# Norms turned by a product with a diagonal matrix of reciprocal roots

## The reference

```python
def rms_norm(x, g):
    x32 = x.astype(jnp.float32)
    y = x32 * lax.rsqrt(jnp.mean(x32 * x32, axis=-1, keepdims=True) + EPS)
    return (y * g.astype(jnp.float32)).astype(x.dtype)

# a layer of the first stack
h = rms_norm(x, norm_mix_pre[l]);  mix = hybrid_mixer(h, ...)
x = x + rms_norm(mix, norm_mix_post[l])
h = rms_norm(x, norm_ffn_pre[l])
x = x + rms_norm(swiglu(h, w_ffn_in[l], w_ffn_out[l]), norm_ffn_post[l])

# a layer of the second stack
x = x + mixer_block(rmsnorm(x, norm_mix[l]), ...)
x = x + cross_attention(rmsnorm(x, norm_xattn[l]), rmsnorm(mem, norm_mem[l]), ...)
x = x + squared_relu_mlp(rmsnorm(x, norm_mlp[l]), w_up[l], w_down[l])
```

## Time and profile before

| | us |
|---|---|
| Runs of the kernel before | 2557.05, 2556.69, 2553.71 (median 2556.69) |
| The profiled execution | 2554.51 |
| Its span, first to last instruction | 2552.4 |
| Mean granted TensorE clock over the span | 0.968 of 2.4 GHz |
| TensorE busy (matmul) | 2371.9, 17164 instructions |
| VectorE busy | 1431.7 |
| ScalarE busy | 1093.0 |
| GpSimd busy | 48.5 |

### The profile page before, as it was taken

One profiled execution on the slowest core, in us unless ns is written; L12 is line 12 of the kernel. 1 busy time (PEld: TensorE's weight loads), 2 busy tenths in 40 slices (PEclk: granted clock), 3 DMA queues, 4 the chain that ended last, 5 costly groups with the idle time before them and its releaser, 6 DMA issues. The chain is left out here.

```text
span 2552.4 us, 40497 instructions
## 1 busy us (share of the span) xinstructions
PE 2371.9 (93%) x17164; PEld 2216.8 (87%) x17164; DVE 1431.7 (56%) x1573; ACT 1093.0 (43%) x1356; POOL 48.5 (2%) x49
## 2 busy tenths in 40 slices
PE   6999998998799999899759999989987999998996
PEld 6988997997798899799659998979966999897985
DVE  6555457444655545644447867454545876744553
ACT  4534444333453354434246433543424643443442
POOL 0000000000000000000000000000000000000000
PEclk9999999999899999999979999999998999998998
DMA  6523355543743336555254434445526443444552
GB/s 201 159 83 110 114 191 165 180 169 114 200 139 93 102 114 198 165 168 197 92 161 125 126 100 146 158 149 165 183 98 188 130 119 100 158 140 148 182 194 78
DMA packets 300001, 370.32 MB, mean 145 GB/s; under 512 B 25006, under 2 KB 267300, under 8 KB 299812
## 3 DMA queue, kind: packets, MB, share of 16 engines
q1 hardware_dynamic: 299812, 367.62, 45.8%
HBM read 366.55 MB, written 1.05 MB: 144 GB/s over the span
## 5 line engine op out<-in xcount | busy, mean ns | idle before, releaser
L400 PE MATMUL ps<-a_nhi,a_wlo 128*128 128x256 f32 x1792 | 525.0, 293 | 12.7 <-DVE a_nlo L953 11.2
L400 PE MATMUL ps<-a_nlo,a_whi 128*128 128x256 f32 x1792 | 508.0, 284 | 0.0
L400 PE MATMUL ps<-a_nhi,a_whi 128*128 128x256 f32 x1792 | 507.9, 283 | 0.0
L923 DVE TENSOR_TENSOR a_wlo<-a_ring,a_whi 128x2048 fp32r<-128x2048 f32 x174 | 395.6, 2286 | 108.3 <-ACT a_whi L707 107.8
L2462 DVE TENSOR_TENSOR b_wlo<-b_ring,b_whi 128x2048 fp32r<-128x2048 f32 (+1 forms) x168 | 379.6, 2263 | 136.2 <-ACT b_whi L2198 136.0
L707 ACT CAST a_whi<-a_ring 128x2048 fp32r<-128x2048 f32 x174 | 331.1, 1905 | 195.3 <-PE ps L400 73.2
L1675 PE MATMUL ps<-b_nhi,b_wlo 128*128 128x256 f32 x1296 | 378.4, 292 | 16.1 <-DVE b_wlo L2462 8.5
L2198 ACT CAST b_whi<-b_ring 128x2048 fp32r<-128x2048 f32 (+1 forms) x168 | 316.2, 1884 | 165.8 <-PE ps L2181 77.4
L1675 PE MATMUL ps<-b_nlo,b_whi 128*128 128x256 f32 x1296 | 369.8, 285 | 0.0
L1675 PE MATMUL ps<-b_nhi,b_whi 128*128 128x256 f32 x1296 | 369.7, 285 | 0.0
L400 PEld LDWEIGHTS ps<-a_nhi,a_wlo 128*128 128x128 f32 x1792 | 345.3, 193 | 18.9 <-DVE a_wlo L923 12.2
(11 more groups left out here) (537 smaller groups left out, 4390.0 us busy)
## 6 DMA issues: line engine op xcount, KB each, us to landing
a_ring<-in_w_in SPq DMA_DIRECT2D x50, 1024.0 KB, 5.2
b_ring<-in_w_in SPq DMA_DIRECT2D x50, 1024.0 KB, 6.1
a_ring<-in_w_ffn_in SPq DMA_DIRECT2D x44, 1024.0 KB, 5.4
a_ring<-in_w_gate SPq DMA_DIRECT2D x32, 1024.0 KB, 5.3
b_ring<-in_w_up SPq DMA_DIRECT2D x32, 1024.0 KB, 5.5
b_ring<-in_w_down SPq DMA_DIRECT2D x32, 1024.0 KB, 5.0
a_ring<-in_w_ffn_out SPq DMA_DIRECT2D x22, 1024.0 KB, 5.0
a_ring<-in_w_branch SPq DMA_DIRECT2D x16, 1024.0 KB, 5.1
```

The lines of the kernel that those rows point to most:

```text
L400: mm = T.matmul(out, w[:, k, c:c + P], x_[:, k, :], start=k == 0 and n == 0, stop=k == KD - 1 and n == 2)
L923: V.tensor_tensor(part(wlo, h), part(ring, h), part(whi, h).bitcast(F32), ALU.subtract).then_inc(lo_ok, 1)
```

## The change

In all 12 norms `xm = x * rstd` is no longer written. VectorE multiplies `ident` by the reciprocal root of each partition's token, which gives a 128x128 diagonal matrix `diag[:, t, :]`, and TensorE multiplies the block of x itself (the stationary operand) by that matrix (the moving one) in an ordinary f32 `matmul`, which turns and scales at once. The memory's norm reads `xm`, which then holds the memory unscaled. Semaphores, waits and the order of the steps are as before; `diag` takes 1 KB a partition in each block.

```diff
--- before.py
+++ after.py
@@ -228,6 +228,7 @@
         nmx, rsum, rinv = at("nmx", [P, 2, 8]), at("rsum", [P, 2, 8]), at("rinv", [P, 8])
         ssq, msq, rstd = (at(n, [P, 5, 4]) for n in ("ssq", "msq", "rstd"))
         nhalf = at("nhalf", [P, 4])
+        diag = at("diag", [P, NT, P])
         assert place[0] <= 229344, place[0]
 
         dst = dict(xbc=xbcp[:, :, 3:SEQ + 3], iqk=iqf, few=iqf[:, 2:4, :],
@@ -387,7 +388,8 @@
                             pe.wait_ge(xn_ok, 2 * e + t + 1)
                             for k in range(KD):
                                 c = (k % 2) * SEQ + t * P
-                                mm = T.transpose(ps[:, 4 * e + k // 2, c:c + P], xm[:, t, k * P:(k + 1) * P], ident)
+                                mm = T.matmul(ps[:, 4 * e + k // 2, c:c + P], x[:, t, k * P:(k + 1) * P], diag[:, t, :],
+                                              start=True, stop=True)
                                 if t and k % 2:
                                     mm.then_inc(tr_ps, 1)
 
@@ -934,7 +936,7 @@
                             mean_square(e, t, 1, D)
                         for t in range(NT):
                             dve.wait_ge(rstd_ok, n_rstd + t)
-                            V.tensor_scalar(xm[:, t, :], x[:, t, :], rstd[:, e, t:t + 1], None, ALU.mult
+                            V.tensor_scalar(diag[:, t, :], ident, rstd[:, e, t:t + 1], None, ALU.mult
                                             ).then_inc(xn_ok, 1)
 
                     def norm_out(e, n_ssq, n_rstd, bank, gain):
@@ -1657,13 +1660,14 @@
                     def both(h):
                         return part(whi, h), part(wlo, h)
 
-                    def turned(r, b0):
+                    def turned(r, b0, src):
 
                         for t in range(NT):
                             pe.wait_ge(xn_ok, 2 * r + t + 1)
                             for k in range(KD):
                                 c = (k % 2) * SEQ + t * P
-                                mm = T.transpose(ps[:, b0 + k // 2, c:c + P], xm[:, t, k * P:(k + 1) * P], ident)
+                                mm = T.matmul(ps[:, b0 + k // 2, c:c + P], src[:, t, k * P:(k + 1) * P], diag[:, t, :],
+                                              start=True, stop=True)
                                 if t and k % 2:
                                     mm.then_inc(tr_ps, 1)
 
@@ -2081,7 +2085,7 @@
                             solution(1)
                         if h == 30:
                             b_turn(3)
-                            turned(1, 4)
+                            turned(1, 4, xm)
 
                     def cross_qk(h):
                         pe.wait_ge(qv_free, h + 1)
@@ -2121,7 +2125,7 @@
 
                     pe.wait_ge(par_in, 128)
                     T.transpose(ps[:, 0, 0:NPAR2], par[:, :], ident[0:NPAR2, 0:NPAR2]).then_inc(par_ps, 1)
-                    turned(0, 4)
+                    turned(0, 4, x)
                     cq_fill(CQA)
                     cq_fill(CQB)
                     for h in range(FEW2, H_OUT2):
@@ -2142,7 +2146,7 @@
                             mm = feature_block(ps[:, 6 + i % 2, m * SEQ:(m + 1) * SEQ], h, m * P, memhi, memlo)
                         mm.then_inc(wk_ps, 1)
                         if i == 1:
-                            turned(2, 0)
+                            turned(2, 0, x)
                     pe.wait_ge(nlo_ok, 12)
                     for i in range(8):
                         h = H_WQ + i
@@ -2160,7 +2164,7 @@
                         residual_part(H_WO + i, i, (qv_free, 8), (ol_ok, i + 1), out_used)
                         if i == 0:
                             cross_pv(3)
-                    turned(3, 4)
+                    turned(3, 4, x)
 
                     for i in range(16):
                         h = H_UP + i
@@ -2466,14 +2470,14 @@
                         V.tensor_scalar(msq[:, e, t:t + n], ssq[:, e, t + at_:t + at_ + n], 1.0 / width, EPS,
                                         ALU.mult, ALU.add).then_inc(msq_ok, 1)
 
-                    def norm_in(e, n_ssq, src):
+                    def norm_in(e, n_ssq):
 
                         for t in range(NT):
                             dve.wait_ge(ssq_ok, n_ssq + t)
                             mean_square(e, t, 1, D)
                         for t in range(NT):
                             dve.wait_ge(rstd_ok, POWER[e, t])
-                            V.tensor_scalar(xm[:, t, :], src[:, t, :], rstd[:, e, t:t + 1], None, ALU.mult
+                            V.tensor_scalar(diag[:, t, :], ident, rstd[:, e, t:t + 1], None, ALU.mult
                                             ).then_inc(xn_ok, 1)
 
                     def turned(r, b0, gain, hi_, lo_, ks=range(KD)):
@@ -2828,7 +2832,7 @@
                                         nhi[:, 2 * h:2 * h + 2, :].bitcast(F32), ALU.subtract).then_inc(ol_ok, 1)
 
                     V.memset(dnp[:, :, 0:3], 0.0).then_inc(pad_ok, 1)
-                    norm_in(0, 1, x)
+                    norm_in(0, 1)
                     dve.wait_ge(par_ps, 1)
                     V.tensor_copy(parT[:, :], ps[:, 0, 0:NPAR2]).then_inc(par_ok, 1)
                     lo(0)
@@ -2919,7 +2923,7 @@
                             turn_lo(2)
                         if 20 <= i <= 25:
                             if i == 23:
-                                norm_in(2, 5, xm)
+                                norm_in(2, 5)
                             if i == 25:
                                 for m in range(4):
                                     gated(1, m)
@@ -2954,7 +2958,7 @@
                     for t in range(NT):
                         residual(0, t)
                     lo(H_WK + 1)
-                    norm_in(6, 7, x)
+                    norm_in(6, 7)
                     lo(H_WK + 2)
                     for i in range(H_WK + 2, H_UP):
                         if i == H_WK + 2:
@@ -2969,7 +2973,7 @@
                     for t in range(NT):
                         residual(1, t)
                     lo(H_UP + 1)
-                    norm_in(7, 9, x)
+                    norm_in(7, 9)
                     turned(3, 4, QL, nhi, nlo)
                     for i in range(H_UP + 1, H_END2):
                         if i + 1 < H_END2:
```

## The result

The changed kernel takes 2560.93 us (median of 20 runs, 2557.35 to 2565.86) against 2556.68 for the kernel before (20 runs, 2552.44 to 2560.35): a ratio of 1.0017 with an interval of 1.001 to 1.0024, that is +4.3 us, between 2.6 and 6.1.

The account below looks back on a forecast made before the run. TensorE, busy 93% of 2552.4 us, was taken as the bound; fillers +5.0, B +2.2, C +1.4 and +0.2, D 0, E -1.3, A -0.5 summed to +7.0, giving 2563.7 us, range 2558.5 to 2569.

Parts of the forecast that it names:

- likeliest case: The forecast itself: the terms sum to +7.0 us, giving 2563.7 us, own range 2561 to 2568; chance 0.60.
- the clock gives everything back: Rival: turns twice as long warm TensorE for each cold block, leaving +4.5 or +2.5 us; chance 0.20.
- A: First norm at 16 us, covered by a weight transfer: no delay, warmer block, -0.5 us.
- E: First norm of layer 1 at 648 us, covered by a weight transfer: no delay, warmer block, -1.3 us.
- C: Low-clock turns on the chain at 1298 and 1928 us, second block's start: +1.4 in layer 0, +0.2 in layer 1.
- main term: Plain f32 product takes two passes, a transpose one: +1.83 us a turn at 2.4 GHz.
- no dearer: Rival: the product runs in one pass like the transpose, only copies count, -1.9 us, 2554.8; chance 0.05.
- four times: Rival: a plain product costs four times a transpose, at fillers and chains, 2592 us; chance 0.04.
- The copy: VectorE's 24 scaled copies of 0.75 us shrink to 284 ns, 0.47 less, on the chain only at B and D.
- Fillers: Memory's and cross norm's turns at full clock between other work: 0.8 and 1.68 us each, twice, sum +5.0.
- B: Low-clock turns on the chain at 438 and 1070 us: ten more passes, less the copy, +1.1 us each.
- D: MLP norm's low-clock turns at 1715 and 2341 us: delay offset by warmer blocks, 0 each, between -2.0 and +1.7.

Follow-up runs that it names:

- experiment 1: Kernel before with its scaled copies kept, transposes replaced by plain f32 products with the unit matrix: 2560.27 us, ratio 1.0015.
- experiment 2: Kernel before with the change only at the memory's and the cross norm's turns: 2558.97 us, ratio 1.0012.
- experiment 3: Changed kernel with transposes of scaled copies kept at the memory's and the cross norm's turns: 2556.24 us, ratio 0.9995.
- experiment 5: Changed kernel with products ordered by pairs of feature blocks, both halves of each pair first: 2559.43 us, ratio 1.0009.
- experiment 4: Kernel before with the change only at the MLP norm's two turns: 2556.09 us, ratio 0.9996.
- experiment 7: Kernel before with unit-matrix transposes in TensorE's idle time, numbers retuned and 26 added behind the MLP's turn: 2541.97 us, ratio 0.9943.
- experiment 6: Kernel before with unit-matrix transposes into unused PSUM banks around the norms, in TensorE's idle time: 2546.46 us, ratio 0.9958.

## Why the prediction was right, and where not

The measured 2560.93 us lies within the range of 2558.5 to 2569.0, 2.8 us below the 2563.7, and a hair under the likeliest case's own 2561 to 2568. By the ratio the change is 0.17% slower, with an interval on both sides of the 0.2% that I took for the bound: I gave "slower" 0.73, and the median falls just into "same", which had 0.25. That the kernel became slower is beyond doubt; that it is by over 0.2% is not. The total stands near the rival "the clock gives everything back" (+4.5), but not by its account: A and E stayed cold in the profile, and C's delay went into a transfer.

**The main term was right.** Two passes for a plain f32 product, read from the 192 records of L1961 for 96 products, came out to the record: 128 and 256. A turn at full clock grew from 1.91 to 3.74 us, +1.83 as predicted. The rivals "no dearer" and "four times" fell with it. The Trainium skill ("TensorE: Matmul & The Clock Gate", Terms) gives transpose mode a factor of four for FP32; here it is two.

**The copy was right.** 282 and 286 ns for the predicted 284, and 0.44 and 0.48 us on the chain at B for 0.47 (experiment 1 against the changed kernel).

**Fillers: 5.0 predicted, 4.3 measured.** 1.59 each for the cross norm's 1.68, since 0.24 us were given back at the next short wait where I had put 0.15; 0.55 each for the memory's 0.8 (experiment 2 and the changed kernel alike). There I had set the whole turn's 1.83 against the 1.03 us of idle time. But that idle time is counted from the end of the turn's last record, which is 0.27 us long, while the next product can start 0.11 behind the start of it: 0.16 more was free. From the turn's first product to the product behind it the trace of before has 1570.62 - 1567.69 = 2.93 us, the changed one 1572.78 - 1569.29 = 3.49: +0.56. That is 0.16 of the missing 0.25.

**B: +1.1 each predicted, 1.77 and 1.39 measured.** The mechanism was right. The mis-sized part is the clock: I let it rise at 441.4 as in the trace before, and it rose behind 443.1, so that the two passes I had put at full clock ran at half speed too (experiment 3, where it rose at 440.8, has 1.25), and I took 0.25 off for what the block would get back, where it had nothing to get: it ran warm before and, from the first product on (its records are 0.36 and 0.28 us long), after.

**C: the step that failed.** "+1.4" for layer 0 took the block's delay for the chain's. Behind the start of the turn the block did come 2.2 us later, but at 1320 TensorE waits for the fourth weight part, whose transfer sets the time:

```profile
1316.10 1.90 ACT L2198 CAST b_whi<-b_ring 128x2048 fp32r<-128x2048 f32 x1 [10.03 <-DMA b_ring<-in_w_in]
...
1320.38 0.58 PE L1675 MATMUL ps<-b_nhi,b_wlo 128*128 128x256 f32 x1 [5.59 <-DVE b_wlo L2462]
```

Before the change it stood idle 5.59 us there until 1320.38, and 2.76 in the changed kernel until 1322.75. ScalarE's cast of that part is released by the DMA in both (1316.10; 1318.46 above), so of a delay of 5.1 us at the block only 2.4 was left. I had looked for what covers A and E, and not looked beyond the first block at C. The 2.4 is no remainder of the turn's delay either: SyncE's queue was 3.17 us late already at its first part of this layer (1292.25 before, 1295.42 after), ahead of the turn, and still 3.17 late when it issued the part in question (1307.34 and 1310.51). The experiments agree. The block at C was put back by 2.2 us in experiments 1 and 3, by 0.9 in 5 and by nothing in 2 and 4, and at the next part the chain stood at +0.2, -0.5, -0.5, -0.6 and -0.3 against the start of the turn: the turn's delay doesn't show there. The -1.3 of the table is this -0.5 and, behind it, 0.8 from the clock, which was low for 5.1 us of that part's products before and for 3.4 after.

In layer 1 the predicted +0.2 was measured as +0.5 for turn and block. In the stretch behind it the clock of the changed kernel's execution fell for 3.4 us (1951.9 to 1955.3), which it had not before; that is 1.5 of the +2.1 there. It fell at that place in experiments 1, 3, 4 and 5 too, among them experiment 4, which has transposes at C. So the +2.1 isn't shown to be a cost of the change.

**D: 0 predicted, -1.15 and -1.05 measured in the profile.** The blocks started 1.7 and 1.3 us late against the predicted 1.66, and gave 2.6 and 2.3 back, the amounts of their cold stretches. But experiment 3 shows the same code with cold blocks and a cost of 0.7 and 1.0, and experiment 2 the code of before with 1.2 and 1.0 gained, so -1.1 is one execution's value, counted against another's; experiment 4 says between -1.6 and +0.7 a place. The 0 was within it.

**E and A: -1.8 predicted, about +0.5 measured in the changed kernel's profile.** E gained 0.5; A lost 1.0, since the clock rose 1.8 us later than before (30.2 for 28.4). In this execution the long turn did not keep TensorE warm over the idle time behind it: the stretches at 24.1 and 658.0 are at 0.50 and 0.53. For E that is not the rule. In experiments 1, 3 and 5, which have the plain products there too, E's block ran at 1.00 (the rows are with the experiments), and E gained 1.5, 1.7 and 1.6 us, where I had put 1.3; in experiments 2 and 4, with transposes at E, it lost 0.3 and 0.2. So the mechanism put for E shows in three of the four profiles with plain products there, and the changed kernel's is the one that misses most of it. Experiment 7 shows that the full clock can be had at both: with transposes in the idle time itself both run at 1.00.

So by the parts: fillers -0.7 against the prediction, B +1.0, C's layer 0 -2.7, D -2.2, E and A +2.3, C's layer 1 with the stretch behind it +2.4. These sum to +0.1, though the profiled pair is 5.9 apart and the forecast was 7.0; the stretches between (-0.35, -0.3) and the start (-0.4) make up the most of the rest. So it was luck that the total fell within the range: in this pair of profiles the clock's terms came out otherwise than put at every place and cancelled. Each such term moves by 1 to 2 us from one execution to another, and a pair of profiles can't tell a forecast of it right or wrong. What stands is the doubled passes, the 6.5 us that they cost, less the copy, at the eight turns where the clock was held, and the net +4.3. Why the clock rises at one time in one execution and 1.8 us later in another stays open; no run here controls it.

## What to carry to other kernels

Count the records of a plain f32 product before putting it in place of a transpose: here each took two passes where the transpose took one, and saving 0.47 us on VectorE cost 1.8 us of TensorE a turn. Before pricing a delay, follow the chain to the next wait on a transfer; it may absorb what the first block shows. Compare stages over several profiles, with and without the change, before giving the clock's part a price: here one place moved by 1 us with no change of its code. Where TensorE stands idle some microseconds ahead of work at half clock, filling that idle time with work of no consequence (here unit-matrix transposes into a free PSUM bank) was worth more than the change under study: 14.6 us of 2557.

## What the runs showed of the hardware that was not expected

- The order in which TensorE was given its work was the bound at B: the 32 passes took 6.7 us, nearly all at 1.2 GHz, and the block started right behind them, though ScalarE had begun its first input 4.3 us before (experiment 5).
- Behind 3.63 us of idle time, through which it stood at 1.00, the clock fell as the block began (experiment 6); behind 2.94 us it stayed up (changed kernel, D), and behind 2.28 and 2.35 us it fell 0.5 and 0.4 us into the block (experiment 3). The length of the idle time alone doesn't say whether it falls.
- Through 56 transposes of the unit matrix, 6.3 us, the granted clock stayed at 1.00 (experiment 7). The Trainium skill ("TensorE: Matmul & The Clock Gate", Part 4: PE-mode transpose) says that the full clock does not engage for transposes; these rows show that it does.
- TensorE's busy time grew by 20.2 us and the kernel's by 4.3; a rise in the busy share (93 to 94%) said nothing of what the change costs.
